# One Trainium2 core, a two-block transformer in fp32: new written orders, broadcast rows of 128 partitions, gates in one pass

## What is computed

```python
i_pre, f_pre = ...                      # 4 + 4 gate columns of h @ w_in
log_i = i_pre + igate_b
log_f = log_sigmoid(f_pre + fgate_b)
# second block
beta = sigmoid(beta_raw)                # 4 columns of h @ mix_w_in
g = -exp(a_log) * softplus(alpha_raw + dt_bias)   # 4 more
q, k = l2_norm(q), l2_norm(k)           # one norm for each head and token
t_mat = a_strict + eye                  # unit lower triangular, per chunk and head
sol = triangular_solve(t_mat, rhs)
```

## Time and profile before

| | |
|---|---|
| median of 3 runs | 1686.4 us (1683.46 to 1686.85) |
| the profiled execution, its own time | 1684.41 us |
| its span (first to last instruction) | 1682.6 us |
| mean granted TensorE clock | 0.969 |
| TensorE / VectorE / ScalarE / GpSimd busy | 1538.8 / 1190.9 / 858.2 / 364.1 us |
| chain that ended last | TensorE 63%, DMA 19%, VectorE 12%, ScalarE 4% |

### The profile page before, as it was taken

How to read it: one execution, slowest core, us unless ns; L and a number is a source line. 1 busy time by engine, 2 the same in 40 slices (tenths; PEclk the granted TensorE clock), 3 DMA queues, 4 the chain that set the end, 5 groups by cost and what they waited for, 6 DMA issues and landing times.

```text
span 1682.6 us, 23795 instructions
## 1 busy us (share of the span) xinstructions
PE 1538.8 (91%) x9208; PEld 1177.4 (70%) x9208; DVE 1190.9 (71%) x2379; ACT 858.2 (51%) x1690; POOL 364.1 (22%) x319
## 2 busy tenths in 40 slices
...
GB/s 279 126 125 126 151 211 93 413 392 413 427 427 426 404 426 426 424 427 399 428 427 426 291 126 101 51 76 128 174 176 151 178 148 103 49 151 178 196 158 146
DMA packets 64336, 419.56 MB, mean 249 GB/s; under 512 B 8160, under 2 KB 12512, under 8 KB 16608
## 3 DMA queue, kind: packets, MB, share of 16 engines
...
...
HBM read 416.96 MB, written 1.05 MB: 248 GB/s over the span
## 4 chain that ended last, share of the span: by engine, by line
PE 63%; DMA 19%; DVE 12%; ACT 4%; issue 1%; POOL 1%; DVEq 0%; POOLq 0%
PE bank L428 62%; DMA uv<-in_uv,idx 18%; DVE lows L499 3%; DVE uv L1579 2%; PE bank L433 1%; ACT acts L440 1%; ACT L440 1%; POOL uv L1728 1%; ACT dg L440 1%; POOL sqT L635 0%; ACT wp L436 0%; DVE cacc L444 0%; DVE t L806 0%; DMA slabs<-in_w_in 0%; DVE cva L444 0%
## 5 line engine op out<-in xcount | busy, mean ns | idle before, releaser
L428 PE MATMUL bank<-uv,dg 128*128 128x512 f32 x1024 | 499.8, 628 | 84.5 <-ACT dg L440 84.4
L428 PEld LDWEIGHTS bank<-uv,dg 128*128 128x128 f32 x1024 | 189.1, 197 | 363.7 <-ACT dg L440 188.8
L1579 DVE CUSTOM_DVE_ANT_0 uv<-uv,htok 128x1024 f32<-128x1024 f32 x256 | 313.1, 1225 | 155.4 <-DMA uv<-in_uv,idx 152.6
L1728 POOL DMA_INDIRECT uv<-in_uv,idx x256 | 299.1, 1168 | 421.1 <-PE bank L428 322.2
L428 PE MATMUL bank<-hn,lows 128*128 128x272 f32 (+2 forms) x704 | 200.9, 285 | 0.0
L499 DVE TENSOR_TENSOR lows<-slabs,wp 128x2048 fp32r<-128x2048 f32 (+1 forms) x75 | 162.4, 2166 | 38.5 <-ACT wp L436 38.2
L440 ACT ACTIVATE acts<-acts,rcol 128x1 f32<-128x1 f32 x256 | 74.2, 290 | 198.1 <-DVE acts L1579 197.4
L436 ACT ACTIVATE wp<-slabs 128x2048 fp32r<-128x2048 f32 (+1 forms) x75 | 134.9, 1799 | 68.2 <-DMA slabs<-in_dn 33.1
L428 PE MATMUL bank<-hn,whl 128*128 128x272 f32 (+2 forms) x768 | 142.1, 286 | 0.0
L635 POOL TENSOR_TENSOR sqT<-sqT 128x272 f32<-128x272 f32 (+1 forms) x35 | 36.1, 1030 | 472.0 <-ACT sqT L440 470.2
L440 ACT ACTIVATE dg<-con,acts 128x128 f32<-128x128 f32 x256 | 102.8, 402 | 60.5 <-PE bank L428 53.3
...
## 6 DMA issues: line engine op xcount, KB each, us to landing
...
```

The costliest lines, as they stand in the source:

```text
L428: ins = T.e.matmul(pr[2] if len(pr) > 2 else out, pr[0], pr[1], start=(start and k == 0), stop=(stop and k == len(pairs) - 1), skip_group_ ...
L1579: V.e.tensor_tensor_reduce(u_, u_, htok[:, n, :], 1.0, 0.0, ALU.mult, ALU.add, acts[:, n, e_:e_ + 1]).then_inc(*V.up("dot", q))
L1728: G.e.indirect_dma_start(uv[q % NU][:, :], None, d["uv"][:, :], bass.IndirectOffsetOnAxis(ap=idx[:, n, e_:e_ + 1], axis=0)).then_inc(s_uv[ ...
```

## The change

The three lists are rewritten, with the same items in another order. The tiles rows, rows2, nrm and nk have 128 partitions instead of 4; GpSimd sets them to zero once, the work goes on in partitions 0 to 3, and `bsel` and its operands take all 128. The gate weights are stored by group, so that one slice of 36 columns holds both groups of a column of x: the first group lands in partitions 0 to 3, the second in 32 to 35. A few waits are added. Nothing in chunk_tensor, chunk_vector, chunk_scalar, chunk_gpsimd or the constants is changed.

```diff
 MIX2_ORDER = """
-pj.w_in2.6.0 unit.0.1 dcols.0.0 pj.w_in2.6.1 unit.0.2 unit.1.0 unit.0.3 unit.1.1 unit.0.4 unit.1.2 ev.w_in2.6.0
...
-pj.w_in2.10.1 kbe.0.0 chunk.2.11 qe.0.0 chunk.0.4 chunk.2.12 z.5.1 ev.w_in2.10.0 xs.1.0 chunk.1.11 chunk.2.13
...
-chunk.2.19 xs.7.0 chunk.1.20 chunk.2.20 chunk.1.21 z.5.0 chunk.2.21 chunk.2.22 pj.w_in2.11.0 chunk.1.22 high.14.0
...
-chunk.1.30 pj.w_in2.12.0 chunk.1.31 ev.w_in2.12.0 chunk.2.31 chunk.0.19 chunk.1.32 chunk.2.32 chunk.0.20 pj.w_in2.13.0
-rec.0.1 pj.w_in2.12.1 ev.w_in2.12.1 rec.0.2 rec.0.3 rec.0.4 rec.1.0 high.15.0 rec.1.1 rec.1.2 pj.w_in2.13.1 low.15.0
...
+unit.1.0 pj.w_in2.6.0 dcols.0.0 unit.0.1 unit.0.2 pj.w_in2.6.1 unit.1.1 bd.0.0 pj.w_in2.7.0 unit.1.2 ev.w_in2.6.0
...
+chunk.2.13 chunk.1.13 high.12.0 xs.1.0 chunk.1.14 pj.w_in2.10.1 chunk.1.15 chunk.2.14 chunk.1.16 chunk.2.15 chunk.0.10
+low.12.0 xs.2.0 chunk.2.16 chunk.0.11 ev.w_in2.10.1 chunk.1.17 chunk.1.18 chunk.2.17 chunk.2.18 high.14.0 chunk.0.12
+chunk.1.19 pj.w_in2.11.0 unit.0.0 chunk.1.20 ev.w_in2.11.0 chunk.2.19 chunk.2.20 chunk.1.21 chunk.1.22 chunk.2.21
+chunk.2.22 high.13.0 chunk.1.23 chunk.0.13 pj.w_in2.11.1 low.13.0 chunk.1.24 chunk.2.23 chunk.1.25 chunk.2.24
+chunk.2.25 high.15.0 chunk.1.26 pj.w_in2.12.0 chunk.0.14 xs.7.0 chunk.2.26 ev.w_in2.11.1 chunk.2.27 ev.w_in2.12.0
...
+chunk.0.18 xs.4.0 chunk.1.30 chunk.0.19 xs.6.0 chunk.1.31 pj.w_in2.13.0 rec.0.1 pj.w_in2.12.1 chunk.2.32 chunk.0.20
+chunk.1.32 rec.0.2 xs.3.0 low.14.0 rec.0.3 low.15.0 rec.1.0 ev.w_in2.12.1 rec.0.4 pj.w_in2.13.1 rec.1.1 ev.w_in2.13.0
...
 MIX_ORDER = """
-mlstm.1.0 mlstm.0.0 mlstm.2.0 mlstm.0.2 mlstm.1.1 mlstm.0.3 mlstm.2.2 mlstm.2.3 mlstm.1.2 stick.4.12 mlstm.2.1
-mlstm.0.1 mlstm.1.3 ahead.w_in.7 mlstm.1.4 pj.w_in.8.0 stick.6.12 mlstm.2.5 mlstm.0.5 mlstm.0.17 mlstm.0.4 mlstm.2.4
...
-pj.w_in.12.1 pj.w_in.9.0 mlstm.2.13 mlstm.3.0 mlstm.2.14 mlstm.2.15 stick.0.0 mlstm.0.15 nm.0 mlstm.3.2 nm.1
...
+mlstm.2.0 mlstm.0.0 mlstm.0.2 mlstm.0.3 mlstm.2.2 mlstm.2.3 pj.w_in.8.0 mem.0 mlstm.0.1 stick.1.11 mlstm.1.0
+stick.3.16 mlstm.0.5 mlstm.0.17 mlstm.1.1 mlstm.1.2 mlstm.1.3 mlstm.2.1 stick.4.12 ahead.w_in.7 mlstm.0.4 mlstm.1.4
...
+mlstm.1.11 mlstm.2.12 mem.1 mlstm.1.12 mlstm.3.0 pj.w_in.12.0 pj.w_in.12.1 stick.2.14 pj.w_in.9.0 mlstm.0.14
...
 SWA_ORDER = """
-pj.sk.0.0 pj.sk.0.1 pj.sv.0.0 kn.flush.0 kn.root.0 kn.rcp.0 pj.sv.0.1 pj.sv.0.2 sq.0.0 kn.bc.0 sq.0.3 sq.0.1 kn.scl.0
...
-att.8.8 att.11.0 att.m0.7 att.11.1 att.7.9 att.m1.2 att.11.3 att.m0.8 att.10.3 att.12.0 att.11.4 att.m1.3 att.8.9
-att.9.5 att.9.6 att.12.1 att.7.10 att.m1.4 att.13.0 att.m0.9 att.10.4 att.m1.5 att.10.5 att.m0.10 att.m1.6 att.13.1
...
+pj.sk.0.0 pj.sk.0.1 pj.sv.0.0 pj.sv.0.1 kn.flush.0 kn.root.0 kn.rcp.0 pj.sv.0.2 sq.0.0 sq.0.3 sq.0.1 sq.0.2 sq.0.4
...
+att.m0.7 att.7.7 att.m1.1 att.11.0 att.8.6 att.9.4 att.6.9 att.6.10 att.m1.2 att.11.1 att.9.5 att.8.7 att.12.0
+att.m1.3 att.7.8 att.7.9 att.10.4 att.m0.8 att.9.6 att.8.8 att.8.9 att.m1.4 att.11.3 att.12.1 att.m0.9 att.11.4
+att.13.0 att.m0.10 att.8.10 att.9.7 att.m1.5 att.14.0 att.10.5 att.7.10 att.13.1 att.m0.11 att.m1.6 att.12.3 att.10.6
...
-            rows = sbuf(ph, "rows", [4, 8, T1])
+            rows = sbuf(ph, "rows", [P, 8, T1])
-            rows2 = sbuf(ph, "rows2", [4, 5, T2])
+            rows2 = sbuf(ph, "rows2", [P, 5, T2])
-            nrm = sbuf(ph, "nrm", [4, 2, T2])
+            nrm = sbuf(ph, "nrm", [P, 2, T2])
-                    nk_ = sbuf(ph, "nk", [4, T2])
+                    nk_ = sbuf(ph, "nk", [P, T2])
         def bsel(h):
-            return C("sel", h * P, h * P + P)[0:4, :]
+            return C("sel", h * P, h * P + P)
+        def gate_pair(g, c):
+            return g[:, :, :, :].rearrange("p a c h -> p (a c h)")[:, 4 * c:4 * c + 36]
...
-            for half in range(2):
-                ins = mm(B[3][0:4, half * T1:half * T1 + T1], [(gates1[:, c, 4 * half:4 * half + 4], XR[:, c, :]) for c in range(NC)])
-                ins.then_inc(*T.up("gates", half))
+            mm(B[3][0:36, 0:T1], [(gate_pair(gates1, c), XR[:, c, :]) for c in range(NC)]).then_inc(*T.up("gates"))
...
             elif s == 5:
+                A.wait_ge(*V.at("t1", h))
...
             elif s == 15 and h % 2:
                 V.wait_ge(*A.at("sroot", h))
+                V.wait_ge(*T.at("lS", p))
...
-            V.e.tensor_tensor(tmp, b[0:4, T1:2 * T1], rsb[0:4, 0:T1], ALU.mult).then_inc(*V.up("gate_raw", 1))
+            V.e.tensor_tensor(tmp, b[32:36, 0:T1], rsb[32:36, 0:T1], ALU.mult).then_inc(*V.up("gate_raw", 1))
...
             G.stage("mix1")
+            G.e.memset(mrow, 0.0).then_inc(*G.up("mrow_zero"))
...
-                        for half in range(2):
-                            hs = slice(4 * half, 4 * half + 4)
-                            mm(B[6 + half][0:4, 16:T2], [(gates2f[:, c, hs], XR[:, c, :]) for c in range(NC)])
-                            mm(B[6 + half][0:4, 0:16], [(gates2[:, c, hs], xT[:, c, 0:16]) for c in range(NC)]).then_inc(*T.up("gates2", half))
+                        mm(B[6][0:36, 16:T2], [(gate_pair(gates2f, c), XR[:, c, :]) for c in range(NC)])
+                        mm(B[6][0:36, 0:16], [(gate_pair(gates2, c), xT[:, c, 0:16]) for c in range(NC)]).then_inc(*T.up("gates2"))
...
                 if h in (1, 2):
                     T.wait_ge(*V.at("unit", 0, h + 1))
+                else:
+                    T.wait_ge(*A.at("uroot", h // 3))
                 T.wait_ge(*V.at("decay", 2))
-                mm(B[2 + h][:, 0:T2], [(bsel(h), bd)]).then_inc(*T.up("bd", h))
+                mm(B[2 + h][:, 0:T2], [(bsel(h), rows2[:, 2, :])]).then_inc(*T.up("bd", h))
...
+                    A.wait_ge(*G.at("nrm_zero"))
...
+                    if c == 3:
+                        for q in range(NC):
+                            V.wait_ge(*V.at("nf", "n", q))
...
+            V.wait_ge(*G.at("rows_zero"))
             scaled_vector(be, B[6][0:4, 0:T2], "an0", T2, np_=4).then_inc(*V.up("be_raw"))
-            scaled_vector(tmp2, B[7][0:4, 0:T2], "an0", T2, np_=4).then_inc(*V.up("dt_raw"))
+            V.e.tensor_tensor(tmp2, B[6][32:36, 0:T2], rsb[32:36, 0:T2], ALU.mult).then_inc(*V.up("dt_raw"))
...
             G.stage("mix2")
+            G.wait_ge(*T.at("an0", "sum"))
+            G.wait_ge(*V.at("gates2_f"))
+            G.e.memset(rows2[:, :, :], 0.0).then_inc(*G.up("rows_zero"))
+            G.e.memset(nrm[:, :, :], 0.0).then_inc(*G.up("nrm_zero"))
...
             G.stage("swa")
+            G.wait_ge(*T.at("pj", "dn0", 15))
+            G.wait_ge(*V.at("gq"))
+            G.e.memset(nk_[:, :], 0.0).then_inc(*G.up("nk_zero"))
```

More of the change, by code:

```diff
@@ L156 @@
-chunk.1.30 pj.w_in2.12.0 chunk.1.31 ev.w_in2.12.0 chunk.2.31 chunk.0.19 chunk.1.32 chunk.2.32 chunk.0.20 pj.w_in2.13.0
-rec.0.1 pj.w_in2.12.1 ev.w_in2.12.1 rec.0.2 rec.0.3 rec.0.4 rec.1.0 high.15.0 rec.1.1 rec.1.2 pj.w_in2.13.1 low.15.0
-rec.1.3 xs.3.0 ev.w_in2.13.0 high.16.0 part.2.0 ev.w_in2.13.1 part.0.0 part.1.0 part.3.0 pj.w_out2.0.0 rec.1.4
-ev.w_out2.0.0 rec.2.0 pj.w_out2.0.1 high.17.0 rec.2.1 ev.w_out2.0.1 pj.w_out2.0.2 rec.2.2 rec.2.3 low.16.0 rec.2.4
-pj.w_out2.0.3 out.0.0 ev.w_out2.0.2 out.0.1 pj.w_out2.1.0 ev.w_out2.0.3 out.0.2 low.17.0 out.0.3 pj.w_out2.1.1
@@ new lines @@
+chunk.0.15 chunk.1.27 chunk.2.28 chunk.0.16 chunk.2.29 chunk.0.17 chunk.1.28 chunk.1.29 chunk.2.30 chunk.2.31
+chunk.0.18 xs.4.0 chunk.1.30 chunk.0.19 xs.6.0 chunk.1.31 pj.w_in2.13.0 rec.0.1 pj.w_in2.12.1 chunk.2.32 chunk.0.20
+chunk.1.32 rec.0.2 xs.3.0 low.14.0 rec.0.3 low.15.0 rec.1.0 ev.w_in2.12.1 rec.0.4 pj.w_in2.13.1 rec.1.1 ev.w_in2.13.0
+part.2.0 rec.1.2 rec.1.3 ev.w_in2.13.1 part.0.0 pj.w_out2.0.0 part.1.0 part.3.0 rec.1.4 ev.w_out2.0.0 high.16.0
+rec.2.0 high.17.0 pj.w_out2.0.1 rec.2.1 low.16.0 ev.w_out2.0.1 rec.2.2 pj.w_out2.0.2 rec.2.3 rec.2.4 out.0.0
@@ L163 @@
+ev.w_out2.0.2 pj.w_out2.0.3 ev.w_out2.0.3 low.17.0 out.0.1 out.0.2 out.0.3 ev.w_out2.1.0 pj.w_out2.1.0 pj.w_out2.1.1
+kbe.0.0 ev.w_out2.1.1 out.0.4 z.5.0 out.0.5 out.0.6 out.0.7 out.0.8 ev.w_out2.1.2 pj.w_out2.1.2 ev.w_out2.1.3
+pj.w_out2.1.3
 """
 MIX_ORDER = """
-mlstm.1.0 mlstm.0.0 mlstm.2.0 mlstm.0.2 mlstm.1.1 mlstm.0.3 mlstm.2.2 mlstm.2.3 mlstm.1.2 stick.4.12 mlstm.2.1
-mlstm.0.1 mlstm.1.3 ahead.w_in.7 mlstm.1.4 pj.w_in.8.0 stick.6.12 mlstm.2.5 mlstm.0.5 mlstm.0.17 mlstm.0.4 mlstm.2.4
-stick.3.16 mlstm.1.5 mem.0 mlstm.0.6 mlstm.1.6 pj.w_in.8.1 mlstm.0.7 mem.6 mlstm.0.8 mlstm.2.6 stick.4.14 mlstm.0.9
@@ new lines @@
+mlstm.1.13 mlstm.2.13 mlstm.2.14 mlstm.0.15 stick.4.16 nm.0 stick.4.13 stick.0.0 mlstm.1.14 nm.1 mlstm.0.16 mlstm.3.2
+mlstm.2.15 mlstm.1.15 pj.w_in.9.1 stick.1.0 mlstm.3.3 nm.2 stick.6.12 stick.0.1 pj.w_in.11.0 stick.2.16 stick.2.0
+stick.5.11 stick.3.0 stick.0.2 mlstm.1.16 mlstm.3.4 stick.0.3 stick.0.4 stick.1.1 stick.3.1 mlstm.3.5 stick.0.11
+stick.0.5 stick.1.2 pj.w_in.11.1 stick.3.2 stick.1.3 stick.3.3 mlstm.2.16 mlstm.3.1 pj.w_in.13.0 stick.3.4 stick.3.5
```

(10 more changed lines are left out.)

135 lines of the change are left out of this document (62 added, 73 removed).

## The result

The changed kernel takes 1655.2 us at the median of four executions (1654.1 to 1656.0), the kernel before 1684.9 beside it: a ratio of 0.9823, 95% interval 0.9806 to 0.984, 29.8 us less. The profiled execution took 1654.1 us.

What follows compares the result with a forecast made beforehand. TensorE was taken to bound the first, delta and attention stages. Terms of 3.5 + 2.3 + 1.45 + 1.6 + 1.7 + 2.3 + 0.8 = 13.65 us off 1684.4 gave 1670.8, or 1672.8 as a median; range 1663 to 1685.

Steps and rivals of the forecast that it cites:

- the gate terms: First stage and delta stage's head: one gate pass instead of two saves 3.5 and 2.3 us.
- ScalarE's table load: Delta stage's head: table loading until 974.50 limits the gate gain; 1.6 of 3.9 us become a longer wait at 988.
- the idle between chunk products: Delta stage: TensorE's idle there should show under 4 us in the profile; it was 5.7 before.
- wrong in kind: All stages together: the prediction's own failure sign, a shrink of under 5 us or over 20.
- the stretch is nearly as bare as before. 0: Attention, between the last sq projection and so.0.0: small products remain, half clock as long as before; 0 us gained.
- rival 3: Attention keeps its full clock, some 8 us more gained, 1664.8 us; chance 0.07.
- the broadcasts in the delta stage: Delta stage: 128-row broadcasts cost nothing themselves and remove the half clock behind those at 1026.63; 1.6 us.
- the first stage: First stage: wide broadcasts save 1.45 us at the first clock fall and 1.7 at 104.1; new order 0.
- The order of the delta stage: Delta stage: new list saves 40% of 5.7 us idle between chunk products, 2.3 us; bounds -5.7 and +5.7.
- Rival 1: Broadcasts: the clock ignores rows and follows gaps; their three terms go, leaving 8.9 us, 1677.5; chance 0.18.
- Rival 2: All three stages: new orders give back time as TensorE waits more; 5.05 us gained, 1681.4; chance 0.12.
- Rival 4: Delta inverses: clock falls among spread small products and stays down; slower, 1690.9 with 30 us of it; chance 0.07.

Runs made afterwards that it cites:

- b_rows: Kernel before with only the 128-row broadcasts and their memsets, old gates and orders; 10.3 us faster than the kernel before, ratio 0.9936.
- a_hold: Changed kernel with useless 128-row products in two TensorE gaps and in each of the attention's last six items; 27.3 us below the kernel before.
- b_gates: Kernel before with only the gates in one pass; 4.8 us faster than the kernel before, ratio 0.9973.
- b_order12: Kernel before with only the new orders of the first and delta stages and their waits; 10.3 us faster than the kernel before, ratio 0.9948.
- b_attn_order: Kernel before with only the attention's new order and the needed waits; 4.2 us faster than the kernel before, ratio 0.9974.
- a_third: The changed kernel run again, nothing altered; 26.9 us below the kernel before.
- a_fill: Changed kernel with useless 128-row products filling three TensorE gaps: first stage, delta stage's head, attention's head; 23.4 us below the kernel before.

## Why the prediction missed

**Right, with their sizes:** the gate terms, 3.5 and 2.3 forecast, 3.4 and 2.2 in the profile and 3.2 and 2.2 alone; that ScalarE's table load holds the second back and 1.6 us turn into a wait; that the memsets cost nothing (the delta stage's head takes 30.39 us with them in b_rows, 30.40 before) and that the inverses are as they were; the idle between chunk products, under 4 us forecast, 4.0 by the window from 1031.55 to 1107 (TensorE busy 71.4 of 75.45). By its own sign the prediction is wrong in kind: it set 20 us as the most that the stages together would shrink by, and the first, the delta stage and the attention shrank by 28.7, gates included.

**The step that failed: "the stretch is nearly as bare as before. 0" for the attention.** 9.7 of the missing 16.6 us are there, and it is rival 3, held at 0.07. The step saw that the new list may cover the 1.31 us wait and still expected the half clock "as long as before, within 4 us", because the products there stay small; it was 3.4 us for 20.2. How long that half clock is differs from profile to profile, and the list changes the odds. Over the profiles in which only the parts above differ, the old list lost 13.7, 13.7, 12.0, 10.2 and 5.1 us to the half clock from the attention on; the new one 1.7 in five, 3.4 in one, and 7.3, 13.8, 15.5 in three more (a_hold's 5.1 aside). By the two exchanges the list is worth 4.2 us at the median in the kernel before and 8.4 in the changed one; what is left of the 9.7 us is the draw of these two profiles. That the wait itself brings the long half clock on fits all five profiles of the old list but was not isolated, so the cause stays open. Without the half clock both lists take 301 to 304 us to the end, so the idle time that the new order saves is not the gain.

**The term mis-sized: the broadcasts in the delta stage.** "the wider operand costs nothing itself" compared durations of the products; the price stands in the gaps beside them, 0.4 us for each group that changes the number of rows. Rows alone gave 5.0 us where 1.6 was booked: 1.7 for the fall at 1029, 1.6 left over for the turns, and 1.7 for the fall at 1121, which the prediction had given to the order. That last one is not surely the rows' either: it is absent from b_gates and b_order12 too, with their 4 rows, and stands in b_attn_order.

**The term mis-sized: the first stage.** Its clock gave 5.1 us for 3.15: the third fall went whole, with the order and the wait for `t` that it removes, and not with the rows (b_rows still has it). The new order gave another 1.2 to 1.4 where 0 was booked, 0.8 of it as idle (TensorE stood for 2.6 us of this piece before, for 1.8 after).

**The order of the delta stage** was sized a little low, 2.3 for 3.3. With the rows and less 1.4 for the new fall behind the idle at 974 that makes 5.0 + 3.3 - 1.4 = 6.9 of the 7.1 measured.

**Rival 1 fell** where it says that the clock ignores rows: with 4 rows a fall at both places in every profile, with 128 rows none, and bursts in a stage that has no idle. That the clock follows gaps as well is true of most other falls here. **Rival 2 too**: the two orders gave 10.3 us alone, 7.2 of them in their own stages. **Rival 4** had the place right and not the price: the new list waits 2.19 us for chunk 0's XX near 1040, and behind that wait the clock falls in 8 of the 11 profiles with that list, for 3.4 us each time. It costs nothing that shows. In a_third the fall is there and the wait for `sqT` that follows in the changed kernel (1.09 us) is gone; in a_fill there is no fall, and that wait stands; the stage takes 157.7 us in both. The gathers' 2.0 us are no effect: with no change in their work VectorE's first to last gathered product lay 655.9 to 664.4 us apart in these runs.
